# Mixture-of-experts decoder on one core: the tokens of an expert's list are put at places 0, 10, 20, ... instead of 0, 1, 2, ...

## The reference

```python
scores = sigmoid(xf @ router_w)                       # (512, 64)
_, idx = top_k(scores + router_bias, 8)               # 8 of 64 experts for each token
gates = scores at idx, divided by their sum, times 2.5
# every expert e, over its own tokens:
y = (silu(h @ w1[e]) * (h @ w3[e])) @ w2[e]           # w1, w3: 1024 x 256, w2: 256 x 1024, float32
out[token] += y * gate
```

## Time and profile before

| | |
|---|---|
| median of 3 runs | 2382.28 us (2380.42 to 2382.53) |
| the profiled execution: its time | 2378.7 us |
| its span, first to last instruction | 2376.9 us |
| busy share of the span: PE, DVE, ACT, POOL | 90%, 67%, 57%, 26% |
| DMA packets, mean rate | 148475, 251 GB/s |
| expert steps, first to last SiLU | 440.2 to 1112.8 us and 1614.3 to 2283.0 us |

### The profile page before, as it was taken

The page is one execution under the profiler, slowest core; times in us unless marked ns, Lnnn a source line. Parts: engine busy times, 40 slices in busy tenths (PEclk is TensorE's granted clock), DMA queues, the critical chain, the costliest instruction groups (busy, mean ns, idle before and its releaser), DMA issues. The chain is left out here.

```text
span 2376.9 us, 31682 instructions
## 1 busy us (share of the span) xinstructions
PE 2134.1 (90%) x10838; PEld 1571.8 (66%) x10838; DVE 1596.6 (67%) x2283; ACT 1353.1 (57%) x1754; POOL 610.4 (26%) x358
## 2 busy tenths in 40 slices
PE   6999999798999999897679999979999999999947
PEld 5788856576676666665367887457766676766633
DVE  2583434797888788786345924248988888888835
ACT  3533721587777777775034356126876777777731
POOL 0012000243333333333311020002433333333323
PEclk9999999899999999999789999999999999999989
DMA  6213043599999999998931230436999999999978
GB/s 197 77 45 151 2 167 125 194 354 346 347 348 337 345 333 336 341 334 297 380 106 54 63 133 3 173 148 249 356 346 345 339 344 338 341 339 339 345 279 333
DMA packets 148475, 595.90 MB, mean 251 GB/s; under 512 B 41957, under 2 KB 68069, under 8 KB 92313
## 3 DMA queue, kind: packets, MB, share of 16 engines
q1 hardware_dynamic: 102264, 527.41, 60.9%
q0 software_dynamic: 46112, 67.23, 9.1%
HBM read 571.23 MB, written 63.46 MB: 267 GB/s over the span
## 5 line engine op out<-in xcount | busy, mean ns | idle before, releaser
L1295 POOL DMA_INDIRECT y_rows<-y,index x128 | 297.0, 2320 | 798.5 <-ACT y L1516 790.0
L1347 PE MATMUL ps_up<-w_hi,rowsT_hi 128*100 128x512 f32 x1024 | 420.6, 411 | 37.3 <-issue 20.4
L1349 PE MATMUL ps_up<-w_hi,rowsT_lo 128*100 128x512 f32 x1024 | 405.8, 396 | 0.0
L1481 ACT CAST w_hi<-w_next 128x2048 fp32r<-128x2048 f32 x128 | 245.7, 1919 | 179.0 <-DMA w_next<-exp_w 169.5
L1481 ACT CAST w_hi<-w 128x2048 fp32r<-128x2048 f32 x128 | 245.3, 1918 | 132.8 <-DMA w<-exp_w 86.6
L1429 DVE TENSOR_TENSOR w_lo<-w,w_hi 128x2048 fp32r<-128x2048 f32 x128 | 292.3, 2285 | 35.9 <-ACT w_hi L1481 35.8
L1429 DVE TENSOR_TENSOR w_next_lo<-w_next,w_hi 128x2048 fp32r<-128x2048 f32 x128 | 292.1, 2282 | 6.3 <-ACT w_hi L1481 6.3
L1372 PE MATMUL ps_y<-w_hi,hiddenT_hi 128*100 128x512 f32 x512 | 211.3, 413 | 70.5 <-issue 66.2
L1347 PEld LDWEIGHTS ps_up<-w_hi,rowsT_hi 128*100 128x100 f32 x1024 | 173.7, 170 | 94.6 <-issue 41.8
L1287 POOL DMA_INDIRECT rows<-x_rows,index x128 | 189.0, 1476 | 122.5 <-issue 61.7
L1349 PEld LDWEIGHTS ps_up<-w_hi,rowsT_lo 128*100 128x100 f32 x1024 | 169.9, 166 | 68.9
(11 more groups left out here) (244 smaller groups left out, 4299.2 us busy)
## 6 DMA issues: line engine op xcount, KB each, us to landing
w_next<-exp_w SPq DMA_DIRECT2D x204, 1024.0 KB, 18.8
w<-exp_w SPq DMA_DIRECT2D x136, 1024.0 KB, 14.2
w_first<-exp_w SPq DMA_DIRECT2D x34, 1024.0 KB, 19.7
w_last<-exp_w SPq DMA_DIRECT2D x32, 1024.0 KB, 19.6
wbuf<-w_in SPq DMA_DIRECT2D x16, 1024.0 KB, 5.5
got<-y_rows SPq DMA_DIRECT2D x8, 2048.0 KB, 23.4
got<-y_rows SPq DMA_DIRECT2D x16, 1024.0 KB, 26.4
w_out_sb<-w_out SPq DMA_DIRECT2D x2, 4096.0 KB, 19.6
```

What stands on the lines that cost most here:

```text
L1295: pool.indirect_dma_start(d["y_rows"], bass.IndirectOffsetOnAxis(ap=index[0:CAP, x.step, 1:2], axis=0), y[0:CAP, x.slot % 2, :], None, bou ...
L1347: pe.matmul(ps_up[b][0:CAP], hi, w_hi, start=(k == 0), stop=False)
L1349: mm = pe.matmul(ps_up[b][0:CAP], lo, w_hi, start=False, stop=(k == KD - 1))
L1481: act.copy(w13_hi[:, :, k, :], w13[x.slot][:, :, k, :]).then_inc(S["up_hi_b" if half else "up_hi_a"], 1)
```

## The change

The constant row `number`, against which the tokens' numbers are compared, is reordered: `number[j]` was j and is now 10 (j mod 10) + floor(j / 10). Token number 0 of a list so goes to place 0, number 1 to place 10, number 2 to place 20, ..., number 10 to place 1, and so on. With n tokens, places 0 to n-1 were filled; now each ten places (0 to 9, 10 to 19, ...) hold a tenth of the tokens, with one more in the first tens where n is not a multiple of ten.

```diff
 CAP = 100
+SPREAD = 10
 MAX_PASSES = -(-SEQ // CAP)
...
-    once = np.concatenate([np.eye(P)[::-1], np.repeat(np.arange(CAP)[None], P, 0), np.ones((P, CAP)), absent], 1)
+    once = np.concatenate([np.eye(P)[::-1], np.repeat(np.arange(CAP).reshape(SPREAD, -1).T.reshape(1, CAP), P, 0), np.ones((P, CAP)), absent], 1)
```

## The result

The kernel with the reordered row takes **2299.95 us** (median of 4 runs, 2298.51 to 2300.17); the kernel before took 2381.35 us beside it (median of 4, 2380.23 to 2382.53). The ratio is 0.9657, 95% interval 0.964 to 0.9674: 3.4% faster, 81 us. Forecast were 2266 us and 116 us, with a range of 2249 to 2308. The direction and the range held; nearly a third of the forecast gain is missing. The profiled execution took 2299.89 us, 78.8 less than the 2378.7 of before.

The account below looks back on a forecast made before the run. Unevenly loaded DMA engines were taken to hold expert steps above PE's 9.67 us; reaching PE's pace saves 121.5 us, less 5 for waits: 116 us off 2378.7, plus 3.6 for the median, 2266 us, range 2249 to 2308.

Parts of the forecast that it names:

- What bounds the kernel: Expert steps: PE's own pace is 9.67 us, transfers take some 10.83 us, and slots loaded ahead hide about ten steps.
- Tens: Gathers and puts: ten places ride on one DMA engine, so 64 rows fill six engines with ten each.
- Always on the same ones: Gathers and puts: each ten places ride on the same engine in every transfer; full engines carry 20 rows a step.
- the rival of 2382 us: Expert steps: no change, because the ten engines move round between transfers or engines slow one another; chance 5%.
- dealt out like cards: Gathers and puts: place j goes to engine j mod 10, so the change packs rows unevenly, 2499 us; chance 3%.
- the cap on the total rate: Expert steps: a total transfer rate holds the step at 10.3 us, 2326 us, a smaller gain; chance 9%.
- The busiest engine's step: Expert steps after the change: weights 7.39 us plus 13.7 rows at 2.11 us on the fullest engine, 9.50 us.
- 0.36 us: Expert steps: today's step exceeds its sum by this; belonging to rows gives 9.75 us after the change, fixed gives 9.86.
- 0.05 us a step: Expert steps: allowance for PE's remaining waits when lists crowd together, 105 x 0.05 = 5 us.
- The dearer row price: Gathers and puts: 0.207 us for 4 KB from the indirect queue's share, giving a 10.23 us step and 2307 us.
- The share of 0.97: Plateau DMA: busy share that reads like sixteen full engines, but overlapping packets on one engine are each counted in full.
- The end of the stage: After the last expert steps: costed at nothing; at most some 6 us a layer come back, for the range only.

Follow-up runs that it names:

- Experiment 2: Indirect transfers name 112 places instead of 100, tokens dealt over the sevens of places, against the kernel before: 2251.73 us, ratio 0.9453.
- experiment 3: 100 places, tokens dealt over the first eight tens of places instead of all ten, against the kernel before: 2337.76 us, ratio 0.9814.
- experiment 4: The kernel before with its list filled from place 99 downwards: 2367.12 us, ratio 0.994.
- experiment 1: Indirect transfers name 112 places instead of 100, the last twelve always empty, old order, against the kernel before: 2341.02 us, ratio 0.983.
- by tens: The changed order with a further 1 MB transfer a step, here with gathers empty and puts alone: 2364.11 us, step 10.69 us.

## Why the prediction came out right, and which of its steps were wrong

**What bounds the kernel: right.** PE's pace is 9.67 us, the transfers are slower, slots loaded ahead hide it for a while. Experiment 2 reaches PE's pace by other places alone.

**Tens: right. "Always on the same ones": wrong.** That ten places ride on one engine was read from 176 packets and five engines in the earlier trace rows, and it holds: 112 places gave 128 packets and a faster kernel in the old order. But the ten engines move round from transfer to transfer, as the strings show. So the rival of 2382 us had the engines right, and the prediction's answer to the rule of a cursor that goes round, "The trace disagrees", is mistaken. The rival's time didn't come all the same, because load that evens out over four steps is still uneven within one transfer. A transfer of weights has landed only when the engine with ten rows has done its share; SP meanwhile waits for a slot, and engines that are ahead run out of packets: 0.79 of 16 before, 0.01 after. The counts are shown; that it is SP's wait which leaves them without work is argued. The places dealt out like cards (2499 us) are refuted by the sign; the cap on the total rate (2326 us) by 380 GB/s.

**The busiest engine's step, 7.39 + 13.7 x 4.096 / 26.6 = 9.50 us, with "9.75" or "9.86" after the 0.36 us that "can't be placed": too small.** This is the term that was mis-sized, and there is no such engine. Measured are 10.19 us (595.7 to 1054.4). Each step past the reserve so lies 0.52 us above PE's pace instead of 0.08 to 0.19. Layer 1 shows what that costs: 45 x 0.52 = 23 us, and its gain is 39.2 instead of 62.7 us. The reserve lasted 15 intervals from 450.7 on (9 before), where "nearly throughout" was said. In both layers 121.5 - 78.4 = 43 us of waiting were left, where "0.05 us a step" had stood for 5.

The sum took for granted that an engine always moves weights at 26.6 GB/s while it moves them, 308 ns for a packet of 8 KB, and rows at 154 ns for 4 KB. The runs show a cost that the change hardly touches: beside gathers the weights' packets are longer, at even and uneven sharing alike. In the kernel after they take 360 ns and the rows 185. A step has 24 packets of weights on each engine, 8.64 us instead of 7.39, and eight rows if even, 1.48 us instead of 1.23. Together that is 10.1 us where the prediction had 8.6 for evenly loaded engines, and since no engine is without a packet any more, it is the whole step: 10.19. Experiment 2 agrees, with 24 x 0.345 + 8 x 0.176 = 9.69 us, about PE's pace: in its second layer (1546.6 to 2159.4, 63 intervals) the step is 9.73 and ACT again waits for weights, 13.8 us between 1800 and 2100.

The 0.36 us would have been a sign, had its two readings been put to more than one kernel. Against the same sum (7.39 us and 0.154 for each row on the fullest engine) the excess on the stretch from 700 to 1000 us is 10.96 - 10.47 = 0.49 with 20 rows, 10.59 - 9.85 = 0.74 with 16 (experiment 3), 10.31 - 9.50 = 0.81 with 13.7. It grows as the load is evened out. Neither "belongs to the rows" nor "fixed" has that form; a sum over all sixteen engines with longer packets has it, since it does not fall as the fullest engine's share does.

**The dearer row price as the upper bound: nearly the result, by luck.** 10.23 us a step and 2307 us stood there, from the indirect queue's own share; 10.19 and 2299.95 came. But 10.23 was worked out for an engine that carries 13.7 rows in every step and moves weights in 7.39 us, and neither is so. That the time fell within the range rests on this bound.

**The share of 0.97 as full engines with idle ones behind it: too much was read into it.** The prediction took overlapping packets to be counted twice, and so had room for engines idle a fifth of the time (8.6 us of 10.83). Overlap is worth 0.06 of an engine in the kernel before, and idle engines 5%. The rest of the time is longer packets: without rows 99.7% + 2.0% go with 26.3 GB/s an engine, with gathers 88.4% + 8.4% with 23.8. A share near 1 doesn't tell spare time either: experiment 2 shows 1.01 while PE waits for nothing.

**The end of the stage: right.** The "some 6 us a layer" were left out of the sum, and 0.2 and 2.0 us came.

**What stays open.** Where gathers and weights collide. Gathers write SBUF, as the weights do, and puts read it. The memory side is unlikely, since without rows 420 GB/s go by at 26.3 GB/s an engine, and packets from memory to memory grow by 1% only beside gathers; but a gather that writes elsewhere wasn't tried, so the place is argued, not shown. The Trainium skill, "DMA: Bandwidth & Descriptors", section "The descriptor swizzle", says that in a transfer to 128 partitions each engine writes partitions of its own, four and four. Gathered tens then write partitions that other engines are writing. No run here shows such a port. Open too is why the same fullness at other places leaves fewer engines without a packet (experiment 4, 0.58 against 0.79), and how much of the gain the rows' wider spread over the partitions has. Seven rows on each of nine engines (experiment 1, 10.59 us) are no better than eight on each of eight (10.59): the packets are shorter, but 1.04 engines are without one. That would follow if a transfer of 112 places, which uses all sixteen engines, put the same places on the same engines each time, so that seven of them never carry rows; this wasn't tested by itself.

## What to carry to other kernels

Where lists don't fill the places of an indirect transfer, ask over how many DMA engines a transfer's places go, and deal the filled places over all sixteen: count the queue's packets for each transfer, take a number of places that is a multiple of 16, and spread the tokens over the engines' blocks (5.5% here, with no instruction saved). Load that evens out over several transfers can still be too uneven within one. Price gathers and puts apart, in a kernel in which the transfers are made to bind, before a sum charges both alike. And where a step exceeds its sum by a few per cent, look whether every packet has grown longer before the excess is spread over the terms.

## What was not expected of the hardware

- A gather of rows into SBUF cost 2.50 us a step, a put of the same rows from it 1.07, and gathers slowed the other transfers from 26.3 to 23.8 GB/s on a busy engine; puts to 25.5, and by tens to 118.91 MB / (0.939 x 4800 us) = 26.4, which is not at all.
- Gathers lengthened the packets of weights, which write SBUF, from 313 to 399 ns, and those from memory to memory by 1%.
- The ten engines of a 100-place transfer move on from transfer to transfer, and evening out the rows within each transfer still gained 3.4%.
- A transfer of 100 places left 176 packets, one of 112 places 128: the larger uses all sixteen engines and has fewer.
- Empty places cost little: with 128 gathers and puts that move no row, the indirect queue took 2.0% of the engines' time, and the rate was 420 GB/s.
